# Tile 0's first two expert heads chosen one at a time, tile 1's query spread, and the context's second norm by blocks

## What is computed

```python
# first block, product-key experts: 8 heads, 16 experts a token and head, out of 16384
q = (hb @ peer_wq).reshape(B, Q_BLOCK, PEER_HEADS, 2, PEER_HALF)
s = einsum('bqhpd,hpnd->bqhpn', q, peer_subkeys)
vals, idx = top_k(s, 16); combo = vals[..., 0, :, None] + vals[..., 1, None, :]
top_s, pos = top_k(combo, 16); expert = take_along_axis(ids, pos); g = softmax(top_s)
a = gelu(einsum('bqhkd,bqd->bqhk', peer_u[expert], hb))
out = einsum('bqhk,bqhkd->bqd', g * a, peer_v[expert])
# second block, start
x   = x   + 0.5 * g1x * swiglu(modulate(rmsnorm(x,   norm_ffn1), sh1x, sc1x), w13_ffn1, w2_ffn1)
ctx = ctx + 0.5 * g1c * swiglu(modulate(rmsnorm(ctx, norm_ffn1), sh1c, sc1c), w13_ffn1, w2_ffn1)
_, kc, vc, ... = project(modulate(rmsnorm(ctx, norm_mix), sh2c, sc2c), w_in)
```

## Time and profile before

| | us |
|---|---|
| median of 3 runs | 1799.28 |
| the runs | 1793.64, 1920.57, 1799.28 |
| the profiled execution | 1795.06 |
| its span | 1793.3 |
| PE, weight loads, DVE, ACT, POOL busy | 1655.2, 1499.4, 1120.9, 642.1, 415.6 |

### The profile page before, as it was taken

How to read it: one execution, slowest core, us unless ns; L and a number is a source line. 1 busy time by engine, 2 the same in 40 slices (tenths; PEclk the granted TensorE clock), 3 DMA queues, 4 the chain that set the end, 5 groups by cost and what they waited for, 6 DMA issues and landing times.

```text
span 1793.3 us, 29482 instructions
## 1 busy us (share of the span) xinstructions
PE 1655.2 (92%) x11948; PEld 1499.4 (84%) x11948; DVE 1120.9 (63%) x1908; ACT 642.1 (36%) x1220; POOL 415.6 (23%) x327
## 2 busy tenths in 40 slices
PE   5999899787898899999995989998999999999997
PEld 3977789777898889999994648998999886989997
DVE  3675547588987497887887762215557448665554
ACT  4444323233332253333012114515444531344442
POOL 0553412354543443443433310000000000000000
PEclk8999899899999999999996999998999999999999
DMA  8678696999999999999998979885355440535442
GB/s 376 235 285 357 272 376 246 414 419 419 400 420 418 416 352 422 421 418 421 420 423 345 400 309 408 317 324 224 112 188 188 186 184 1 188 149 224 177 158 92
DMA packets 58307, 542.71 MB, mean 303 GB/s; under 512 B 6464, under 2 KB 6592, under 8 KB 7744
## 3 DMA queue, kind: packets, MB, share of 16 engines
q1 hardware_dynamic: 21168, 271.37, 38.2%
q0 software_dynamic: 37008, 269.50, 36.9%
HBM read 539.80 MB, written 1.05 MB: 302 GB/s over the span
## 4 chain that ended last, share of the span: by engine, by line
PE 58%; DMA 22%; DVE 10%; issue 6%; ACT 1%; POOL 1%; SPq 0%; POOLq 0%; DVEq 0%; ACTq 0%
PE psum L476 58%; DMA arena<-in_experts,idx_stage 17%; DVE arena L2217 3%; DMA ring<-in_w_ada 2%; DMA arena<-in_w_ada 1%; DVE arena L2206 1%; DMA ring<-in_w_ffn 1%; DMA ring<-in_w_out 1%; DMA ring<-in_w_in 1%; POOL arena L1207 1%; DVE arena_r L1806 0%; POOL idx_stage L1200 0%; DVE ring_r L1740 0%; DVE x_t L2138 0%; DVE arena L2328 0%
## 5 line engine op out<-in xcount | busy, mean ns | idle before, releaser
L2206 DVE CUSTOM_DVE_ANT_0 arena<-arena 128x1024 f32<-128x1024 f32 x256 | 313.8, 1226 | 144.2 <-DMA arena<-in_experts,idx_stage 138.2
L1207 POOL DMA_INDIRECT arena<-in_experts,idx_stage x256 | 302.5, 1182 | 353.5 <-DVE arena L2217 154.2
L476 PE MATMUL psum<-h_t,ring 128*128 128x128 f32 (+1 forms) x2064 | 330.7, 321 | 18.9 <-ACT h_t L1531 14.0
L476 PEld LDWEIGHTS psum<-h_t,ring 128*128 128x128 f32 x2064 | 300.8, 193 | 47.1 <-ACT h_t L1531 14.4
L1740 DVE TENSOR_TENSOR ring_r<-ring,ring_r 128x1024 fp32r<-128x1024 f32 (+1 forms) x172 | 207.3, 1213 | 189.5 <-ACT ring_r L1256 188.6
L476 PE MATMUL psum<-small,arena 128*128 128x128 f32 x2080 | 258.4, 287 | 50.0 <-ACT small L1611 50.0
L476 PEld LDWEIGHTS psum<-small,arena 128*128 128x128 f32 x2080 | 252.8, 203 | 55.2 <-ACT small L1611 54.6
L476 PE MATMUL psum<-small_r,ring_r 128*128 128x256 f32 x1600 | 289.0, 284 | 4.1 <-DVE h_t_r L1827 4.1
L476 PEld LDWEIGHTS psum<-small_r,ring_r 128*128 128x128 f32 x1600 | 247.7, 191 | 6.7 <-issue 6.7
L1256 ACT ACTIVATE ring_r<-ring 128x1024 fp32r<-128x1024 f32 (+1 forms) x172 | 179.1, 1047 | 170.0 <-PE psum L476 153.7
L476 PE MATMUL psum<-arena_r,ring_r 128*128 128x256 f32 x1552 | 227.5, 282 | 2.8 <-DVE arena_r L1806 2.8
(11 more groups left out here) (259 smaller groups left out, 1571.8 us busy)
## 6 DMA issues: line engine op xcount, KB each, us to landing
ring<-in_w_ffn SPq DMA_DIRECT2D x35, 2048.0 KB, 11.6
ring<-in_w_in SPq DMA_DIRECT2D x31, 2048.0 KB, 8.7
ring<-in_w_ada SPq DMA_DIRECT2D x25, 2048.0 KB, 10.3
ring<-in_w_ffn SPq DMA_DIRECT2D x24, 1408.0 KB, 7.7
arena<-in_w_ada SPq DMA_DIRECT2D x5, 2048.0 KB, 13.9
ring<-in_w_out SPq DMA_DIRECT2D x4, 2048.0 KB, 8.7
ring<-in_peer_wq SPq DMA_DIRECT2D x4, 2048.0 KB, 12.7
ring<-in_p_ret SPq DMA_DIRECT2D x4, 2048.0 KB, 7.5
```

The source lines that it names most:

```text
L476: return nc.tensor.matmul(o, a, b, start=first, stop=last)
L1207: nc.gpsimd.indirect_dma_start(rows[slot % GBUF], None, dram["experts"], bass.IndirectOffsetOnAxis(ap=idx_stage[:, slot:slot + 1], axis=0) ...
L2206: step(nc.vector.tensor_tensor_reduce(u, u, h2[:, n // PER_TILE, :], 1.0, 0.0, ALU.mult, ALU.add, dots[:, n % 8, s:s + 1]), sem("dots"))
```

## The change

Three edits.

1. The heads are chosen in blocks given by `HEAD_BLOCKS`: tile 0's blocks are 1, 1, 2, 2 and 2 heads, tile 1's four of two. Each block's indices are published when they are known. Everything counted by blocks (`combined`, `best`, `gates`, `choice_made`) follows. The context's gather moves from ahead of the second list to ahead of the fourth.
2. Tile 1's query is planned at five chunks in six batches from batch 0 on, 19 by batch 22, instead of 8 at once and one a batch. The context starts at batch 29 instead of 24, and in tile 1 its plan has 114 chunks instead of 119 over the same 61 batches.
3. The context's second norm goes by blocks. ACT squares each 256-column block after its output slab, into buffers of its own (`sq_ctx`), and PE adds it to a sum bank held apart. Output slabs 5 to 7 do the context first and keep their slab; tile 0's products on them (`fx_y5` to `fx_y7`) follow, with the last block of squares behind `fx_y5`. ACT takes the root straight from the sum bank, DVE makes the reciprocal and multiplies by block, ACT scales and shifts by block, and PE's `kc0` waits for each block by itself. The five chunks without work are gone.

```diff
@@ -57,12 +57,14 @@
 PER_TILE = SLOTS // BATCH
 BATCHES = NT * PER_TILE
 ALONE, HELD = 2, 2
-QUERY_FIRST, QUERY = 8, 19
-CTX_START = 24
-CTX_FIRST, CTX_SECOND = QUERY + 5 + 4 * ALONE, 127 - 4 * ALONE
+LATER = 5
+QUERY = 19
+CTX_START = 29
+CTX_FIRST, CTX_SECOND = QUERY + 5 + 4 * ALONE, 122 - 4 * ALONE
 CTX_LAST = PER_TILE - 3
+HEAD_BLOCKS = [[1, 2, 4, 6, 8], [2, 4, 6, 8]]
 BLOCK_STEPS = 5
-CHOICE_FIRST, CHOICE = BLOCK_STEPS + 2, 2 * (BLOCK_STEPS * PH // 2 + 1)
+CHOICE_FIRST, CHOICE = BLOCK_STEPS + 2, sum(BLOCK_STEPS * len(ends) + 1 for ends in HEAD_BLOCKS)
 ROUND = 16
 
 
@@ -181,7 +183,7 @@
 def context_due(n):
 
     if n < CTX_START:
-        return min(QUERY_FIRST + n, QUERY)
+        return min((n + 1) * 5 // 6, QUERY)
     if n < PER_TILE:
         return QUERY + min(n + 1 - CTX_START, PER_TILE - 4 - CTX_START) * (CTX_FIRST - QUERY) // (PER_TILE - 4 - CTX_START)
     return CTX_FIRST + min(n + 1 - PER_TILE, CTX_LAST) * CTX_SECOND // CTX_LAST
@@ -195,6 +197,11 @@
 def choice_made(step):
 
     return next(n for n in range(PER_TILE) if choice_due(n) >= step)
+
+
+def block_heads(g):
+
+    return slice(([0] + HEAD_BLOCKS[0])[g], HEAD_BLOCKS[0][g])
 
 
 def program(nc, dram, out):
@@ -280,6 +287,9 @@
         hid_first = first_home[:, 1024:1024 + KF * P].rearrange("p (k t) -> p k t", k=KF)
         rstd_first = first_home[:, 3840:3968]
         F0, G0 = 5120, 11264
+        sq_ctx = ([arena[:, 4096 + i * L:4096 + (i + 1) * L] for i in range(4)]
+                  + [arena[:, F0 + 5632 + i * L:F0 + 5632 + (i + 1) * L] for i in range(2)]
+                  + [small[:, i * L:(i + 1) * L] for i in range(2)])
         T0 = G0 + 8192
 
         iq_t = arena[:, G0:G0 + 1024].rearrange("p (j t) -> p j t", j=4)
...
@@ -893,6 +903,11 @@
 
                 squares(tag, hid_c, KD)
                 done_at["ss_" + tag] = at[0]
+
+            def add_squares(bank, k):
+
+                pe.wait_ge(sem("sq_ctx2"), k + 1)
+                return mm(psum[:, bank, 0:L], ones[:], sq_ctx[k], k == 0, k == KD - 1)
 
             def ctx_hidden(i, w):
 
...
@@ -984,17 +1000,39 @@
                         last = mm(o[:, 0:L], w[:, k, :], hid_c[:, k, :], k == 0, k == KF - 1)
                         if k in (7, 15, KF - 1):
                             yield
-                    if i == 0:
-                        pe.wait_ge(*emptied(f"fx_b{ALONE - 1 if ALONE else 10}"))
+                    if i < LATER:
+                        if i == 0:
+                            pe.wait_ge(*emptied(f"fx_b{ALONE - 1 if ALONE else 10}"))
+                        for k in range(KF):
+                            last = mm(o[:, L:L + P], w[:, k, :], hid_first[:, k, :], k == 0, k == KF - 1)
+                    else:
+                        later.append((i, w, used[0] - 1))
+                    ctx_end(f"fc_y{i}", last)
+                    if i < LATER:
+                        release()
+                        yield
+                    if i == 1:
+                        at_bank[0] %= len(cycle)
+                        sum_bank = cycle.pop(at_bank[0])
+                        pe.wait_ge(*tenant[sum_bank])
+                    if i > 1:
+                        add_squares(sum_bank, i - 2)
+                add_squares(sum_bank, KD - 2)
+                for i, w, n in later:
+                    o = begin(f"fx_y{i}", "dve")
                     for k in range(KF):
-                        last = mm(o[:, L:L + P], w[:, k, :], hid_first[:, k, :], k == 0, k == KF - 1)
-                    ctx_end(f"fc_y{i}", last)
-                    release()
+                        last = mm(o[:, 0:P], w[:, k, :], hid_first[:, k, :], k == 0, k == KF - 1)
+                    ctx_end(f"fx_y{i}", last)
+                    release(n=n)
+                    if i == LATER:
+                        last = add_squares(sum_bank, KD - 1)
+                        at_bank[0] %= len(cycle)
+                        cycle.insert(at_bank[0], sum_bank)
+                        at_bank[0] += 1
+                        begin("ss_ctx2", "act", sum_bank)
+                        ctx_end("ss_ctx2", last)
                     yield
-                ctx_squares("ctx2")
-                for _ in range(5):
-                    yield
-                pe.wait_ge(sem("h_ctx2"), KD)
+                need = {k: (sem("h_ctx2"), k + 1) for k in range(KD)}
                 for i in range(4):
                     if i % 2 == 0:
                         w = next_slab("w_in_2", 2 + i // 2).rearrange("p (k n) -> p k n", k=KD)
@@ -1002,6 +1040,8 @@
                     for j in range(2):
                         c = i % 2 * 256 + j * P
                         for k in range(KD):
+                            if k in need:
+                                pe.wait_ge(*need.pop(k))
                             last = mm(o[:, j * L:(j + 1) * L], w[:, k, c:c + P], h_t[:, k, :], k == 0, k == KD - 1)
                         if j:
                             ctx_end(f"kc{i}", last)
@@ -1209,10 +1249,11 @@
                             bass.IndirectOffsetOnAxis(ap=idx_stage[:, slot:slot + 1], axis=0),
                         ).then_inc(row_landed[slot % GBUF], 16)
 
-            lists = [(t, b0 * 2 * PSEL // ROUND, b1 * 2 * PSEL // ROUND) for t in range(NT)
+            lists = [(t, b0 * PSEL // ROUND, b1 * PSEL // ROUND) for t in range(NT)
                      for b0, b1 in zip([0] + published[t], published[t])]
+            ctx_at_list = published[0].index(4) + 1
             for known, (t, r0, r1) in enumerate(lists):
-                if known == 1:
+                if known == ctx_at_list:
 
                     pool.wait_ge(sem("lane"), 1)
                     pool.wait_ge(group_done, index["ks1_3"] + 1)
@@ -1222,8 +1263,11 @@
                 if t and r0 == 0:
                     one_round(t, 0, 0)
                     r0 = 1
-                with pool.Fori(0, r1 - r0) as r:
-                    one_round(t, r0, r)
+                if r1 - r0 == 1:
+                    one_round(t, r0, 0)
+                else:
+                    with pool.Fori(0, r1 - r0) as r:
+                        one_round(t, r0, r)
 
 
         @block.scalar
@@ -1539,9 +1583,9 @@
                                          (copy_h, 1, 1, "ht1_1"), (copy_scores, 1, 3, "ks1_3")):
                     yield done_at[name] + 1
                     copy(t, i)
-                yield choice_made(BLOCK_STEPS * PH // 2) + 1
+                yield CTX_START + 2
                 act.wait_ge(sem("ctx_landed"), 16)
-                act.wait_ge(sem("combined"), PH // 2)
+                act.wait_ge(sem("combined"), len(HEAD_BLOCKS[0]))
                 square("ctx1", hid_c, ctx_t, KD)
                 yield from context_norm("ctx1", mod2_v[:, 0, :, 1])
 
...
@@ -1580,10 +1624,16 @@
                     yield from first_hidden(i)
                 for i in range(ALONE):
                     yield from first_hidden(i)
-                yield done_at["fc_y7"] + 2
-                act.wait_ge(*emptied("fc_y7"))
-                square("ctx2", hid_c, ctx_t, KD)
-                yield from context_norm("ctx2", mod2_v[:, 3, :, 1])
+                for i in range(KD):
+                    yield done_at[f"fc_y{i}"] + (2 if i < KD - 1 else 1)
+                    act.wait_ge(*emptied(f"fc_y{i}"))
+                    nc.scalar.activation(sq_ctx[i], ctx_t[:, i, :], ACT.Square).then_inc(sem("sq_ctx2"), 1)
+                yield done_at["ss_ctx2"] + 1
+                norm_root("ctx2")
+                for k in range(KD):
+                    act.wait_ge(sem("normed_ctx2"), k + 1)
+                    nc.scalar.activation(h_t[:, k, :], h_t[:, k, :], ACT.Identity, bias=mod2_v[:, 3, k:k + 1, 1],
+                                         scale=scale_of["ctx2"][:, k:k + 1]).then_inc(sem("h_ctx2"), 1)
                 for i in range(4):
                     yield done_at[f"kc{i}"] + 1
                     copy_out(f"kc{i}", flat(kc_t[:, 2 * i:2 * i + 2, :]))
...
@@ -1613,7 +1663,8 @@
 
             def gate_and_diagonal(n):
 
-                act.wait_ge(sem("gates"), min(n * BATCH // (2 * PSEL), PH // 2) + 1)
+                ends = HEAD_BLOCKS[0]
+                act.wait_ge(sem("gates"), 1 + (len(ends) if n >= PER_TILE else sum(n * BATCH >= end * PSEL for end in ends)))
                 act.wait_ge(sem("gelus"), n + 1)
                 for g in range(BATCH * n, BATCH * (n + 1)):
                     weigh(g)
...
@@ -2068,40 +2119,42 @@
-                two = [P, 2, PSEL, PSEL]
-                for g in range(PH // 2):
-                    v.wait_ge(*emptied(f"ks{t}_{g}"))
-                    for hp in (4 * g, 4 * g + 2):
+                for g, h1 in enumerate(HEAD_BLOCKS[t]):
+                    h0 = ([0] + HEAD_BLOCKS[t])[g]
+                    v.wait_ge(*emptied(f"ks{t}_{h0 // 2}"))
+                    for hp in range(2 * h0, 2 * h1, 2):
                         top16([(key_s[t][:, n, :], top_v[:, n, :], fv[:, n, :]) for n in (hp, hp + 1)])
```

(34 more changed lines are left out.)

40 lines of the change are left out of this document (22 added, 18 removed).

## The result

| | before | after |
|---|---|---|
| median, us | 1793.64 (7 runs, lowest 1790.04) | 1778.72 (7 runs, 1772.73 to 1782.81) |
| span of the profiled execution, us | 1793.3 | 1776.4 |
| ratio, 95% interval | | 0.9919 (0.9900 to 0.9938) |

The changed kernel is 0.8% faster, 14.5 us by the ratio; 1779 was predicted. The question is whether it got there by the steps of the prediction. One of the seven executions before took 1920.57 us, far above the other six, and the ratio leaves it out.

What follows compares the result with a forecast made beforehand. The DMA engines bound the gather phase at 420 GB/s. PE's path saves 11.3 + 2.5 + 2.0 = 15.8 us and the DMA's 2.0 + 6.9 + 7 = 15.9, so 1795.06 - 16 = 1779 us, range 1765 to 1799.

Steps and rivals of the forecast that it cites:

- The start, 3.5 us, 2.0 by the end: Start: loss against 420 GB/s falls from 24.4 to 21.0 us, 3.5 saved; batch 31 takes back 1.5.
- the dot comes at about 268.4: Start, DVE: first dot at about 268.4 us instead of 271.20, a pair of top 16 being moved or gone.
- 5.0 us a batch: Batches 6 to 22: PE's rows and chunks need 5.0 us a batch, as does the DMA; no loss, no room.
- Rival (a): Start pays nothing and batch 31 costs 4 us, with 14 gained behind it: 1785 us; chance 0.20.
- The norm on PE's path, 11.3 + 2.5: Second norm, PE: `kc0` starts 11.3 us earlier, with up to 2.5 us more from half clock not met.
- So `kc0` starts at 967.3: Norm, PE: `fx_y6` and `fx_y7` cover the norm, so `kc0` starts at 967.3 instead of 978.57, 11.3 us.
- up to 2.5 us more for half clock not met: Behind the norm, PE: 128 instructions take 28.1 us at the faster pace instead of 30.46.
- The first `kc` matmul released by a DMA: Behind the norm, PE: sign of being wrong, the first `kc` product waiting for its slab; no size given.
- rival (c): Norm: held slots release late, the stall stays and 15 us of slab loads follow it: 1808 us; chance 0.08.
- Rival (d): Norm not covered: PE waits as long at blocks 6 and 7 as at the norm before: 1791 us; chance 0.14.
- The DMA's path, 2.0 + 6.9 + 7: DMA: 2.0 us from the start, 6.9 round the norm, 7 at the end, 15.9 in all.
- At the end the last dot no longer waits for `vc7`: End of gathers: last dot freed from ACT's copy of `vc7`, 7 of 8 us between DMA and PE, range 0 to 9.

Runs made afterwards that it cites:

- e1: Kernel before with only the start's edits (two one-head blocks in tile 0, spread query, context from batch 29), old norm: ratio 0.9992.
- e7: Changed kernel with LATER = 6: two of tile 0's products behind the context's instead of three, two slabs held: 1772.70 us, ratio 0.9888.
- e9: Changed kernel with LATER = 7: only tile 0's last output product left behind the context's, so none covers the norm: ratio 0.9950.
- e10: Changed kernel with the context's chunks spread over the first 58 of tile 1's 64 batches, not 61: ratio 0.9934.
- e2: Kernel before with only the norm's edit (by blocks, tile 0's last products behind it, turn at batch 122), old start: ratio 0.9938.
- e5: Changed kernel with the first gather held until the last but one `spare_w` slab for the start has landed: ratio 0.9922.
- e12: Changed kernel with four query chunks ahead of the first row and LATER = 6: 1768.72 us, ratio 0.9886.

## Why the prediction was right, and where it was not

**The start, 3.5 us, 2.0 by the end.** Right. The steps "ids near 238.5" and "the dot comes at about 268.4" came out as 238.99 and, in the traces in which the clock fell ahead of the slab, as it had in the kernel before (e1, the second of the changed kernel and e7), 267.82, 266.13 and 266.81. The first dot's gain of 2.8 us is exact in relation to the fifth gather. The ninth gather gained 3.15, not 4.3: two rows behind the idle stretch took 5.2 to 6.3 us (5.5 was said), and POOL's copy of the indices 0.9 to 1.2 instead of 0.19. From the fifth gather to batch 64 the six traces with both edits as they are in the change (it twice, e1, e7, e9, e10) took 366.2 to 369.1 us, mean 367.9, the kernel before and e2 370.1 and 369.5: 1.9 us on average, and 1.5 from the earlier mark at 208 to 212 us (mean 413.1 against 414.6 us, the six within 2.3 of each other). e1's ratio says 1.4 (-0.5 to 3.4). So a gain of nothing isn't ruled out by the ratio alone.

In between the lead is larger, and it goes again: batch 20 starts at 391.0 us in the kernel before and at 375.6 in the changed one, batch 24 at 411.1 and 412.5. The context's first three slabs, 6.29 MB, were issued at 322.62 us before and at 377.64 after. Until then gathers had the DMA to themselves, and then the slabs took it back. These slabs are also what the prediction left out of "5.0 us a batch" for batches 6 to 22: it was 6.2 us a batch before and 6.1 in the changed kernel, and as both have them, the difference didn't suffer. (Its 11 + 4 chunks there are one more than the 14 it names.) The wait of PE of "some 4 us" at batch 31 is there, 3.99; what of it reaches batch 64 wasn't separated. Rival (a), that the start pays nothing, seemed shown by the changed kernel's first trace; the late mark and the place where the clock fell had only hidden the gain there.

**The norm on PE's path, 11.3 + 2.5.** The mechanism was right, its size 3 us too large. From batch 64 to the last dot the four kernels with the old norm took 441.4 to 443.4 us (mean 442.5), and the changed kernel twice, e2 and e5 took 430.8 to 432.5 (mean 431.7): 10.8 of 13.8 us. The step that failed is "So `kc0` starts at 967.3": it starts at 968.73, since its slab isn't there, and in relation to batch 64 9 to 11 us earlier than in the four traces of the old norm (352.1 to 354.0, now 343.2). The term of "up to 2.5 us more for half clock not met" measured 0.9: 128 products took 29.58 us instead of 30.46. PE still stands before them, 2.1 to 2.5 us, and the window behind has this clock:

```profile
968.70:972.00 3.30, 3.27 (x9) 2.66 (x10) 3.19 (x6) 0.00 (x0) 2.02 (x2) 0.60 0.96 410
```

Once e7 and e12 took the wait away, the clock stayed up (in e2 it did so behind a wait of 2.33 us, too). The first `kc` matmul released by a DMA was one of the prediction's own signs of being wrong. The held slots of rival (c) did have a price, then: some 4 us directly, the wait and the clock, and not 15, since `fx_y5` wasn't late; e7, which holds one slab fewer, is 6.3 us shorter over the stretch. Rival (d) is out: nothing waits at blocks 6 and 7.

**The slab beside the gathers.** It was issued at 956.38 and the first product on it ran at 968.73, 12.3 us later, as in the earlier trace rows. From 950 to 975 us the two queues (columns: packets, MB, share of 16 engines) had the engines nearly half and half:

```profile
q0 software_dynamic: 721, 5.24, 52.7%
q1 hardware_dynamic: 331, 4.90, 46.1%
```

The rule of the Trainium skill, DMA: Bandwidth & Descriptors, section Queues, rings and completion order, that an engine takes turns between its queues agrees with these rows.

**The DMA's path, 2.0 + 6.9 + 7.** This was wrong as an account, though its sum was only some 3 us too large. "At the end the last dot no longer waits for `vc7`" failed: ACT still waits 5.61 us for PE ahead of each of the last copies, up to the one at 1053.28. That end paid 1 to 2 us (last gather to last dot 19.6 us before, 18.0 and 18.9 after), not 7, though 6.8 us of DVE's waits were there to be had, of which e7 and e12 take 6.0, while the gathers gained 9.4 in tile 1 (batch 64 to the last gather: 422.2 to 423.8 us with the old norm, 412.8 to 414.1 with the new), not 6.9. I had treated PE and DMA as two paths whose ends could be compared. They are tied batch by batch through ACT and DVE, as e10 shows. That the second sum came out that near is partly luck: one term was 5 to 6 us too large and another 2.5 too small.

**The sum.** 1.9 + 10.8 = 12.7 us by the traces, 14.5 and 16.1 by the two ratios (intervals 11.1 to 17.9 and 13.5 to 18.8), 16 predicted. So 1779 was right within what can be measured, with a norm 3 us too large. That the profiled pair hit it to the microsecond is luck: of its 16.9 us 11.7 lie between batch 64 and the last dot and 6.2 in the tail, untouched code, and 1.0 was lost up to batch 64. The two groups of the runs fit such chances of some 5 us, which the two traces of the changed kernel show at the start alone; no trace here tells which run had which.

## What to carry to other kernels

Take the difference between two traces in stretches, from marks that both have, with one mark ahead of anything that the change touches, and get a second trace of the same kernel before an early stretch is explained. Here a mark that lay 4 us later by chance, and a clock that fell in one place instead of another, looked like a failed edit. When a wait has grown, look first whether the waiting engine came sooner: the slab was never late. Look for an engine that has waited and is then on the path: work put into that wait is free and keeps the clock up. A buffer that is held to cover a wait has its own price, in the load that could not be issued. With no cover, one product and two (0, 4.9 and 9.8 us) the stretch from batch 64 to the last dot took 435.0, 425.4 and 431.7 us: take the shortest cover that is long enough.
